# Two softmax layers: the next unit's scores in the middle of a dense piece instead of behind the transposes

## The reference, cut to what matters

```
# first block, second layer (512 frames are 8 chunks, so all earlier frames are in reach)
s = einsum('bhtd,bhjd->bhtj', qi, kb) + bias
p = softmax(where(mb, s, NEG_INF));  o = einsum('bhtj,bhjd->bhtd', p, vb);  y = o @ w_out
# second block, second layer
logits = einsum('bhqd,bhkd->bhqk', q, k) * scale + cumf[q] - cumf[k]
probs = softmax(where(mask, logits, -inf));  o = (probs @ v) * silu(g);  y = o @ w_out
```

## Time and profile before

| | |
|---|---|
| median of 3 runs | 1866.33 us (1865.37 to 1877.03) |
| profiled execution, span | 1867.6 us |
| PE busy | 1796.5 us (96%), 9203 matmuls |
| DVE, ACT, POOL busy | 1203.8, 764.2, 805.5 us |
| first softmax layer, its units | about 730 to 882 us |
| second softmax layer, its units | about 1671 to 1825 us |
| mean granted TensorE clock | 0.984 of full |

### The profile page before, as it was taken

How to read it: one execution, slowest core, us unless ns; L and a number is a source line. 1 busy time by engine, 2 the same in 40 slices (tenths; PEclk the granted TensorE clock), 3 DMA queues, 4 the chain that set the end, 5 groups by cost and what they waited for, 6 DMA issues and landing times. The chain is left out here.

```text
span 1867.6 us, 25054 instructions
## 1 busy us (share of the span) xinstructions
PE 1796.5 (96%) x9203; PEld 1456.2 (78%) x9203; DVE 1203.8 (64%) x1775; ACT 764.2 (41%) x1205; POOL 805.5 (43%) x577
## 2 busy tenths in 40 slices
PE   5999999899999999999998999999999999999999
PEld 4776677788888877877787888888888887877877
DVE  5786557977766563564488677777488845346662
ACT  2443346222222253554351232233544456665551
POOL 3433235655665354221365556653532334442222
PEclk8999999999999999998999999999999999999999
DMA  9633525545555333221256555542221132332211
GB/s 344 203 121 116 169 91 176 173 158 169 174 179 165 112 112 102 69 79 47 68 185 219 167 173 166 165 142 90 91 89 51 46 92 90 98 88 80 85 37 68
DMA packets 126780, 235.77 MB, mean 126 GB/s; under 512 B 8256, under 2 KB 37824, under 8 KB 126688
## 3 DMA queue, kind: packets, MB, share of 16 engines
q1 hardware_dynamic: 123648, 227.17, 37.3%
q10 hardware_dynamic: 3040, 7.34, 1.1%
HBM read 232.36 MB, written 2.13 MB: 126 GB/s over the span
## 5 line engine op out<-in xcount | busy, mean ns | idle before, releaser
L2346 POOL TENSOR_TENSOR wsp<-raw,wsp 128x512 fp32r<-128x512 f32 x528 | 797.5, 1540 | 1042.2 <-ACT wsp L189 1042.2
L231 PE MATMUL bank<-xT,wsp 128*128 128x512 f32 x2592 | 601.6, 391 | 6.3 <-ACT xT L367 4.2
L231 PEld LDWEIGHTS bank<-xT,wsp 128*128 128x128 f32 x2592 | 486.3, 188 | 111.4 <-issue 3.9
L189 ACT ACTIVATE wsp<-raw 128x2048 fp32r<-128x2048 f32 x132 | 252.8, 1915 | 512.5 <-PE bank L478 229.5
L478 PE MATMUL bank<-wsp,hT 128*128 128x512 f32 x1344 | 321.3, 399 | 11.1 <-DVE htmp L606 11.1
L478 PEld LDWEIGHTS bank<-wsp,hT 128*128 128x128 f32 x1344 | 256.7, 191 | 72.2 <-DVE htmp L606 12.0
L231 PE MATMUL bank<-wsp,xT 128*128 128x512 f32 x1248 | 301.9, 397 | 2.2 <-POOL wsp L2346 2.0
L231 PEld LDWEIGHTS bank<-wsp,xT 128*128 128x128 f32 x1248 | 232.2, 189 | 56.0 <-issue 4.5
L589 DVE TENSOR_TENSOR h<-h 128x512 f32<-128x512 f32 x64 | 62.8, 996 | 79.6 <-ACT h L546 79.6
L1367 PE MATMUL bank<-xT,wsp 128*128 128x512 f32 x384 | 100.3, 405 | 0.0
L606 DVE TENSOR_TENSOR htmp<-bank,gate 128x512 f32<-128x512 f32 x96 | 65.9, 686 | 46.2 <-PE bank L478 46.2
(11 more groups left out here) (309 smaller groups left out, 2142.5 us busy)
## 6 DMA issues: line engine op xcount, KB each, us to landing
raw<-in_ff_w SPq DMA_DIRECT2D x64, 1024.0 KB, 5.4
ada_ring<-in_w_ada SPq DMA_DIRECT2D x48, 384.0 KB, 3.7
ada_ring<-in_ada_w SPq DMA_DIRECT2D x48, 384.0 KB, 3.7
ring<-in_w_ada SPq DMA_DIRECT2D x64, 256.0 KB, 3.4
raw<-in_odd_w_in SPq DMA_DIRECT2D x16, 1024.0 KB, 5.5
raw<-in_gla_w_in SPq DMA_DIRECT2D x12, 1024.0 KB, 7.1
raw<-in_att_w_in SPq DMA_DIRECT2D x12, 1024.0 KB, 5.2
raw<-in_even_w_in SPq DMA_DIRECT2D x12, 1024.0 KB, 5.2
```

What stands on the lines that cost most here:

```text
L189: act.activation(wsp[:, slot, 0], raw[:, slot], ACT.Copy).then_inc(hi_made, 1)
L231: mm = pe.matmul(out_ap, l, r, start=(start and n == 0), stop=(stop and n == 2))
L2346: ins = pool.tensor_tensor(wsp[:, slot, 1, k], raw[:, slot, k], wsp[:, slot, 0, k].bitcast(F32), ALU.subtract)
```

## The change

In each iteration that has a dense piece, the scores of the next unit are issued in the middle of the piece (at step `(k0 + k1) // 2`), instead of behind T of unit `u`-1. No instruction is added or taken away, and ACT, DVE, POOL and SP keep their lists. It takes place in 27 iterations of the first layer and in 31 of the second (the last unit has no successor).

```diff
-        def pe_slot_piece(pe, name, ts, piece, first_free):
+        def pe_slot_piece(pe, name, ts, piece, first_free, inside=None):
...
             for k in range(k0, k1):
+                if k == (k0 + k1) // 2 and inside:
+                    inside()
...
                 if u in work:
-                    pe_slot_piece(pe, name, ts, work[u], v_made + (1 if name == "att_in" else 2))
+                    pe_slot_piece(pe, name, ts, work[u], v_made + (1 if name == "att_in" else 2),
+                                  (lambda: scores(u + 1)) if u + 1 < NU else None)
                 if u not in work and u + 1 < NU:
                     scores(u + 1)
...
                     mm.then_inc(s["tr"], 1)
-                if u in work and u + 1 < NU:
-                    scores(u + 1)
                 if u >= 2:
```

## The result

| | before | changed |
|---|---|---|
| median of 10 runs each, us | 1867.37 (1862.29 to 1877.03) | 1878.99 (1870.48 to 1880.74) |
| ratio, 95% interval | | 1.0052 (1.0038 to 1.0066) |
| span of the profiled execution | 1867.6 | 1874.7 |

The change makes the kernel slower by 0.52%, which on 1867.37 is 9.7 us (7.1 to 12.3). The direction was forecast, the size was 4.1: less than half. Put on the median that stood before the forecast, 1866.33, the ratio gives 1876.0; the median of the ten runs itself lies 1 us above the range's upper end.

A forecast was written before the change was run, and what follows sets the result against it. TensorE's list was taken as the bound; 4.6 - 10.2 + 4.3 + 2.5 + 1.9 + 1.05 = +4.1 us on the median 1866.33 gave 1870.4 us, range 1863 to 1878 us for 8 in 10.

The forecast's parts named there:

- What bounds the kernel: Both softmax layers: TensorE, busy 96% of the span, sets the time through the order of its list.
- The waits that go: T waiting for VectorE's norm in both layers: earlier scores give it room, -10.2 us, bounds 0 and -10.2.
- 1.6 left over: First layer: T's norm wait at 877.13, behind the dense pieces, keeps its order and its 1.6 us.
- The waits that come: TensorE waiting for ScalarE's copy, gate tiles' bank 6 and bank 7: +4.3, +2.5, +1.9 and +1.05 us.
- Copies: Scores waiting for ScalarE's copy behind high halves and gate tiles: +4.3 us first layer, +2.5 second.
- Bank 7: V of unit 8, iteration 10, waits 1.65 for L1817 behind the gate multiplication, where 0.6 was: +1.05 us.
- Gate tiles: The next tile's first piece waits for the gate multiplication to free bank 6, iteration 3 longest: +1.9 us.
- The switch: Dense matmuls to half-height scores and back inside each piece: 0.08 a time, 58 splits, +4.6 us.
- The high bound that I took: Entering scores in a piece, the matmul ahead fully run out first: 0.15 for each of 58, 8.7 us.
- The sign: Whole kernel: slower, by +4.1 us; chances faster 0.01, within 1% 0.97, slower 0.02.
- The clock rival: TensorE's clock drops for one more stretch after longer idle time near iteration 27: 5.1 more, 1875.5 us; chance 0.12.

The follow-up runs named there:

- Scores behind the piece: Kernel before, with the next unit's scores issued behind the whole dense piece and ahead of T, no piece broken: 1867.2 us, ratio 1.0002.
- with the high half late: Next unit's scores behind the whole dense piece and ahead of T, ScalarE making the high half behind the copy: 1862.78 us, ratio 0.9961; again 1863.47, 0.9979.
- only 14 early iterations and the high half late: Kernel before, scores ahead of T in 14 of 58 iterations, elsewhere behind T; ScalarE's high half behind the copy: 1862.57 us, ratio 0.9968.

## Why the forecast was right in sign and short in size

- **What bounds the kernel: right.** TensorE's list sets the stages; what was added to it came out in the total. By the forecast's own sign the size was wrong in both stages: each was to end 1 to 4 us longer, and they ended 6.1 and 4.4 longer.
- **The waits that go: right.** -10.2 was forecast with 1.6 left over. The price left out the wait at 1677, which would have made it -10.8. Waits for the norm fell from 10.3 to 2.8: besides the 1.6, the second unit's norm kept 0.8 us of its wait in the first layer and 0.4 in the second (in the first, VectorE has no idle time from the first norm, at 727.90, to the second, at 733.82).
- **The waits that come: right by place, somewhat too large.** Copies: forecast 4.3 and 2.5 more, found 5.3 more all told (4.8 + 2.0 against 1.5), a fifth less. Iteration 27 waits 2.04 where 2 was said. Bank 7: 1.65 said, 1.66 found. Gate tiles: 0.25 to 0.68 said, six waits and 1.9 in all; six found, 1.2 in all. Rows after, first the scores of 28, then V of unit 8:

```profile
857.58 0.55 PE L1447 MATMUL bank<-akr,aqr 64*128 64x128 f32 x6 [2.04 <-ACT aPT L1526]
...
1723.68 0.44 PE L1488 MATMUL bank<-fPT,tok 128*64 128x128 f32 x4 [1.66 <-DVE gT L1818]
```

- **The switch: mis-sized, and this is the miss.** "The extra is 0.08 a time; 27 + 31 splits x 0.08 = +4.6 us" counted the entry into the scores and took the way back as free, by comparing what follows the scores with what follows V. But the price of coming back is not between the scores and the first dense matmul; it is between the first and the second, 0.34 instead of 0.23. Single starts give 0.09 for the entry and 0.11 for the restart, 0.20 x 58 = 11.6 us. With that the forecast's own sum is 11.6 - 10.2 + 4.3 + 2.5 + 1.9 + 1.05 = 11.2, and 10.5 with the wait at 1677, against 10.5 in the stages. So close an agreement is partly luck: copies and gate tiles came out 2.2 below their terms, the norms kept 1.2 more than was said, and up to 1.7 of the first stage is clock. The restart could have been read in the rows: nine dense matmuls took 2.19 to the next start, 0.243 each, and the twelve at 746.98 took 2.86, 0.238 each. Three more cost 0.67 and not 0.72, so a run had a fixed part. The high bound that I took, 8.7, left it out too.
- **The sign: by a small margin.** The waits that come (9.75) and those that go (10.2) nearly cancel in the forecast, so that its sign hung on the switch alone. That term was real and larger than forecast, so the sign was not luck.
- **The Trainium skill,** page "TensorEngine Tiling (Array Packing)", section "Key Properties", says that changing the tiling mode drains the engine. The trace agrees in kind: a break by the same shape cost 0.13 us in the rows, little more than its own matmul, and one by the half-height shape 0.22 beyond its own time, with a part on the way in and a part on the way back.
- **The clock rival: seen, not as the cause.** In the first layer, behind the longer wait of iteration 27, the clock was at its lower level from 860 to 869 (0.50, which is 1.2 of 2.4 GHz), and a second, shorter stretch came from 876 on. The columns are length, busy us per engine, granted clock, DMA share, GB/s:

```profile
860.00:869.00 9.00, 9.00 (x47) 7.78 (x49) 2.58 (x8) 1.71 (x6) 2.36 (x2) 0.50 0.35 117
859.00:871.00 12.00, 12.00 (x73) 10.30 (x73) 3.56 (x11) 3.57 (x10) 3.36 (x3) 0.57 0.26 87
876.00:881.00 5.00, 5.00 (x23) 3.89 (x24) 1.05 (x3) 0.96 (x3) 0.00 (x0) 0.66 0.00 0
```

  Before, there was one stretch of 10.3 us at 0.50, which lost 5.15; the first one here lost the same (0.43 of 12.00). The one from 876 on accounts for 1.7 us (0.34 of 5.00) of the 6.1 here at most. The second layer lost 4.4 with its clock at 1.00 throughout:

```profile
1674.00:1827.00 153.00, 147.75 (x1163) 115.72 (x1162) 95.91 (x274) 81.59 (x191) 34.09 (x26) 1.00 0.20 65
```

## What to carry to other kernels

Where TensorE is the bound, count changes of matmul shape, not instructions, and count them net: what the move adds less what it removes. Here a half-height group inside a dense run turned three changes an iteration into four, 0.15 to 0.2 us each time and some 10 us in all, while the waits only changed places. Between the dense piece and T, which have the same shape, the group adds a change as well, but a cheaper one (0.15 where the middle costs 0.20, both by rows); only a border where the shape changes anyway adds none. Price a change to the second matmul behind it, by comparing runs of different lengths, not only to the first. And before moving work off a wait, list what the moved group itself covered: here it was the cover of three other kinds of wait.

## What the runs showed that was not expected

- A full-height matmul in the middle of a dense run costs 0.13 us, little more than itself (0.11); a half-height pair costs 0.22 more than itself. In the stages both look cheaper, for added work also shortens waits.
- VectorE's scaling took 1.75 us instead of 0.62 while GpSimd ran; more than half of the norm's waits in the kernel before stand behind such a case, which fits that moving ScalarE's high half gained nothing there (ratio 0.9994).
- The clock behind the dense pieces of the first layer: nearly the same lists lose 3 us or not. Scores behind the piece had it at 0.80 and 0.75 in the stretches 850 to 862 and 862 to 873; with the high half late it was full in the first and 0.84 in the second:

```profile
850.00:862.00 12.00, 10.97 (x102) 8.78 (x101) 7.00 (x23) 7.70 (x17) 5.33 (x4) 1.00 0.09 16
```

  Its waits for the copy there are 1.0 us in three pieces of at most 0.4 instead of one of 1.0. That was so in two profiles of one kernel; what keeps the clock up was not tested. The late high half is not enough: with only 14 early iterations and the high half late the clock was 0.79 and 0.77 in these stretches.
